# Group norms of a two-block forward pass: sums on all partitions, one chain per four groups, scales spread by single-pass matmuls

## The chip, the cores and the metric

The kernel runs on one core of a Trainium2 chip. The metric is the device time of one execution in microseconds (us). Before the change the median of three runs is 2449.47 us (2449.28 to 2449.51).

## What is computed

The reference runs a first transformer block (hybrid mixer and SwiGLU) and a second one on 256 tokens of width 2048, all in float32. Only one piece of the first block is touched by the change, the group norm behind the mixer:

```python
attn = forgetting_attention(q, k, v, log_f)            # 8 heads of 128
conv = gate_b * short_conv(gate_c * hc, conv_w)        # 8 groups of 128
y = jnp.concatenate([attn, conv], axis=-1).reshape(Bsz, L, N_GROUPS, GROUP_DIM)
y = rmsnorm(y, out_gain.reshape(N_GROUPS, GROUP_DIM)).reshape(Bsz, L, D_MIX)
return y @ w_out
# rmsnorm: y * rsqrt(mean(y * y, -1) + 1e-6) * gain
```

So each of 16 groups of 128 features needs, for each of 256 tokens, the mean of 128 squares, one over its root, and a product with it, before `w_out` can use the group.

## The kernel before, in words

Features lie on the 128 partitions and tokens on the free axis. `ytile[:, g, :]` is group g (heads are groups 0 to 7, the convolution's groups 8 to 15) as 128 features x 256 tokens. A sum over a group's features is therefore a sum over partitions, which TensorE makes by a matmul with ones.

**The dense products.** Every weight matrix streams through the ring `raw` (5 slots) in units of 128x1024. ScalarE rounds a unit to fp32r as `w_hi` (`split_hi`, L895), VectorE makes the rest `w_lo` (`split_lo`, L1307); both rings have 4 slots (`SPLIT`). A product is then made of single-pass fp32r matmuls of the two parts (L614 to L623). A product of a block of four output tiles is cut into *steps*: one unit for one of the four tiles (`product_step`), here 1536 or 1548 columns. In a step of "pair" tiles each second kind of matmul has 512 columns (L614, L618), in a step of "conv" tiles all have 258 (L621 to L623). Six PSUM banks (`out_bank`) take the tiles.

**The order of the rest** is written by hand as step numbers. Each engine's program walks through the steps; in step s it first does the work of the products (splits, evictions) and then what `rms`, `first_mixer` and so on hang on that step. Step numbers below count from CONV0, the first step of the convolution's products. Head hd has its scores at step 16 hd, its first and second transposes of the probabilities ("p0" and "p1", L703, L706) at 16 hd + 14, its product with v at 16 hd + 23 (L713 to L718). In `attention`, VectorE adds the masks and reduces (L1435 to L1442) one step behind the scores, ScalarE takes the exponentials (L958) three steps behind them, VectorE normalises (L1446, L1450) five behind.

**Side banks.** All these small matmuls write to two PSUM banks in turn. `take_side(kind, key, sem_free, value)` hands them out in program order; whoever takes a bank waits until the one that took it two places earlier has been read out:

```python
i = len(side_release)
if i >= 2:
    t_.wait_ge(*side_release[i - 2])
```

**The group norm before.** ScalarE squares a group (L981) into one of two buffers (`square_buf`) at `square_step[g]`. Three steps later TensorE sums it: two fp32 matmuls per group, with the squares as the stationary operand and one column of ones moving (L725), which leaves 128 tokens on the partitions x 2 columns. VectorE scales them into `gms` (L1454) a step later. When four groups have their sums, a *call* (`group_calls`, at a fixed step) makes the roots of all four at once on 128x8 elements: reciprocal (L1464), square root on ScalarE (L986), a Newton step in four small operations (`polish`, L1339 to L1345) two steps behind. Since the scales then lie with tokens on partitions, they are turned back in two *pairs* of groups: VectorE makes four diagonal 128x128 tiles (L1492), TensorE multiplies ones with them (four fp32 matmuls, L734) so that every partition has the scale of every token, VectorE multiplies `ytile` by that (L1473), ScalarE and VectorE split the result for `w_out` (L991, L1479). The four calls stand at steps 77, 108, 146 and 200; the spreads of their pairs (L734) 7 and 11 steps behind.

## Time and profile before

| | |
|---|---|
| median of 3 runs | 2449.47 us |
| profiled execution | 2449.89 us, its span 2447.8 us |
| TensorE matmul busy | 2433.8 us, 99% of the span |
| VectorE busy | 1614.5 us, 66% |
| ScalarE busy | 1202.2 us, 49% |
| GpSimd busy | 173.9 us, 7% |
| DMA engines, mean | 184 GB/s |
| TensorE clock granted, mean | 1.0 |
| spreads L734 | 64 records, 235.5 to 349.6 us |
| sums L725 | 64 records, 182.7 to 338.1 us |

Times count from the start of the span. An fp32 matmul stands as two records, an fp32r matmul or a transpose as one. Matmuls are pipelined and their ends are modelled, so what a piece of work costs TensorE is read from start to start. A difference of about 0.2% (4.9 us) is what a measurement of this kernel can tell from none.

### The profile page before, as it was taken

How to read it: one execution, taken by the hardware profiler on the slowest of the kernel's cores; microseconds unless marked ns; L12 is line 12 of the kernel's file. 1: busy time of each engine (PE TensorE's matmuls, PEld its weight loads, DVE VectorE, ACT ScalarE, POOL GpSimd, SP SyncE). 2: the span in 40 equal slices, each digit the busy share in tenths (PEclk: the TensorE clock that was granted, in tenths of full speed). 3: DMA queues.
4: the chain of work that ended last, by engine and by line, in shares of the span. 5: the costliest groups of instructions: out<-in, count | busy, mean ns of one | idle time of the engine just before them, and what ended most of it. 6: DMA issues, size and time to landing. Idle time of an engine off the chain costs nothing.

```text
span 2447.8 us, 36417 instructions
## 1 busy us (share of the span) xinstructions
PE 2433.8 (99%) x14762; PEld 2173.7 (89%) x14762; DVE 1614.5 (66%) x2518; ACT 1202.2 (49%) x1728; POOL 173.9 (7%) x195
## 2 busy tenths in 40 slices
PE   8999999999999999999999999999999999999999
PEld 8999998888888888888888888888998888888887
DVE  5646676676666666667677756678885665565667
ACT  6545545544544543455555654544554443443544
POOL 0001111000000000002211102031110000000010
PEclk9999999999999999999999999999999999999999
DMA  7554456666566666665655455565566666656663
GB/s 250 180 161 139 141 165 189 200 184 194 182 198 190 189 190 189 192 190 185 197 188 167 166 185 190 184 193 186 162 196 193 189 189 189 194 190 189 183 193 117
DMA packets 125751, 449.59 MB, mean 184 GB/s; under 512 B 13840, under 2 KB 16400, under 8 KB 125584
## 3 DMA queue, kind: packets, MB, share of 16 engines
q1 hardware_dynamic: 125296, 446.91, 58.8%
q8 instruction: 116, 1.90, 0.3%
q14 instruction: 51, 0.42, 0.0%
q10 hardware_dynamic: 288, 0.36, 0.0%
HBM read 445.12 MB, written 2.10 MB: 183 GB/s over the span
## 4 chain that ended last, share of the span: by engine, by line
PE 96%; DVE 2%; ACT 1%; issue 0%; DMA 0%; ACTq 0%
PE out_bank L614 28%; PE out_bank L618 27%; PE out_bank L615 14%; PE out_bank L617 14%; PE out_bank L622 3%; PE out_bank L621 3%; PE out_bank L623 3%; DVE w_lo L1307 1%; ACT w_hi L895 0%; PE side_bank L734 0%; PE side_bank L694 0%; PE side_bank L749 0%; PE side_bank L725 0%; DVE h L1824 0%; DMA h<-in_tokens 0%
## 5 line engine op out<-in xcount | busy, mean ns | idle before, releaser
L1307 DVE TENSOR_TENSOR w_lo<-raw,w_hi 128x1024 fp32r<-128x1024 f32 x839 | 1037.4, 1240 | 601.0 <-ACT w_hi L895 596.9
L895 ACT CAST w_hi<-raw 128x1024 fp32r<-128x1024 f32 x840 | 878.1, 1049 | 953.6 <-PE out_bank L618 874.8
L614 PE MATMUL out_bank<-a_op,w_hi 128*128 128x512 f32 x1984 | 784.2, 395 | 0.5 <-DVE h L1334 0.3
L618 PE MATMUL out_bank<-a_op,w_hi 128*128 128x512 f32 x1984 | 776.7, 391 | 0.0
L615 PE MATMUL out_bank<-a_op,w_lo 128*128 128x256 f32 x1984 | 558.8, 282 | 0.0
L617 PE MATMUL out_bank<-a_op,w_lo 128*128 128x256 f32 x1984 | 552.0, 278 | 0.0
L617 PEld LDWEIGHTS out_bank<-a_op,w_lo 128*128 128x128 f32 x1984 | 380.1, 192 | 84.3
L615 PEld LDWEIGHTS out_bank<-a_op,w_lo 128*128 128x128 f32 x1984 | 372.9, 188 | 77.0
L614 PE MATMUL out_bank<-b_op,w_hi 128*128 128x512 f32 x992 | 389.7, 393 | 0.0
L618 PE MATMUL out_bank<-b_op,w_hi 128*128 128x512 f32 x992 | 388.0, 391 | 0.0
L614 PEld LDWEIGHTS out_bank<-a_op,w_hi 128*128 128x128 f32 x1984 | 373.1, 188 | 2.0 <-DVE w_lo L1307 0.7
L618 PEld LDWEIGHTS out_bank<-a_op,w_hi 128*128 128x128 f32 x1984 | 373.0, 188 | 0.0
L615 PE MATMUL out_bank<-b_op,w_lo 128*128 128x256 f32 x992 | 279.7, 282 | 0.0
L617 PE MATMUL out_bank<-b_op,w_lo 128*128 128x256 f32 x992 | 275.8, 278 | 0.0
L617 PEld LDWEIGHTS out_bank<-b_op,w_lo 128*128 128x128 f32 x992 | 190.4, 192 | 42.0
L615 PEld LDWEIGHTS out_bank<-b_op,w_lo 128*128 128x128 f32 x992 | 186.3, 188 | 39.9
L614 PEld LDWEIGHTS out_bank<-b_op,w_hi 128*128 128x128 f32 x992 | 186.5, 188 | 0.0
L618 PEld LDWEIGHTS out_bank<-b_op,w_hi 128*128 128x128 f32 x992 | 186.5, 188 | 0.0
L1324 DVE TENSOR_TENSOR work<-work,out_bank 128x256 f32<-128x256 f32 x248 | 102.4, 415 | 119.0 <-ACT work L914 118.3
L621 PE MATMUL out_bank<-a_op,w_hi 128*128 128x258 f32 (+1 forms) x504 | 146.5, 291 | 0.0
L622 PE MATMUL out_bank<-a_op,w_hi 128*128 128x258 f32 (+1 forms) x504 | 144.2, 286 | 0.0
L623 PE MATMUL out_bank<-a_op,w_lo 128*128 128x258 f32 (+1 forms) x504 | 143.8, 285 | 0.0
(302 smaller groups left out, 1974.6 us busy)
## 6 DMA issues: line engine op xcount, KB each, us to landing
raw<-in_w_ff SPq DMA_DIRECT2D x256, 512.0 KB, 4.2
raw<-in_w_in SPq DMA_DIRECT2D x223, 512.0 KB, 3.7
raw<-in_w_gu SPq DMA_DIRECT2D x176, 512.0 KB, 4.2
raw<-in_w_down SPq DMA_DIRECT2D x88, 512.0 KB, 4.3
raw<-in_w_out SPq DMA_DIRECT2D x64, 512.0 KB, 4.3
raw<-in_w_ba SPq DMA_DIRECT2D x16, 512.0 KB, 3.9
raw<-in_w_bp SPq DMA_DIRECT2D x16, 512.0 KB, 3.8
out<-h SPq DMA_DIRECT2D x8, 256.0 KB, 2.3
```

The source lines that it names most:

```text
L614: t_.e.matmul(bank[:, :], wh, a_both, start=start, stop=False, skip_group_check=True)
L615: mm = t_.e.matmul(bank[:, 0:SEQ], wl, a_hi, start=False, stop=stop, skip_group_check=True)
L617: t_.e.matmul(bank[:, 0:SEQ], wl, a_hi, start=False, stop=False, skip_group_check=True)
L618: mm = t_.e.matmul(bank[:, :], wh, a_both, start=False, stop=stop, skip_group_check=True)
L621: t_.e.matmul(to, wh, a_hi, start=start, stop=False, skip_group_check=True)
L622: t_.e.matmul(to, wh, a_lo, start=False, stop=False, skip_group_check=True)
L623: mm = t_.e.matmul(to, wl, a_hi, start=False, stop=stop, skip_group_check=True)
L895: a.e.copy(w_hi[:, m % SPLIT, :], raw[:, u % RAW, :]).then_inc(hi_split)
L1307: v_.e.tensor_tensor(w_lo[:, m % SPLIT, :], raw[:, u % RAW, :], w_hi[:, m % SPLIT, :].bitcast(F32), ALU.subtract).then_inc(lo_split)
L1324: v_.e.tensor_tensor(y, y, bank_of(tile)[:, 0:SEQ], ALU.add).then_inc(bank_free)
```

## The change

The sum of a group is now one fp32 matmul with ones stationary and the 256 squares moving, so that all 128 partitions hold the sum of every token. VectorE scales 32 of the partitions into `group_ms`: the four groups of a call lie on partitions 0 to 31, 32 to 63, and so on. The chain of a call (reciprocal, square root, Newton step) runs on 128x256 elements, and two more operations split the scales into two fp32r parts, `scale_hi` and `scale_lo`. The diagonal tiles are gone: a pair is spread by four fp32r matmuls of 256 columns, whose stationary operand is one column of `group_pick` (a one on partition 0, 32, 64 or 96) repeated 128 times. Heads are summed 8 steps behind their square instead of 3; the first call moves from step 77 to step 82, the other three stay. A buffer for the DMA queues of GpSimd is made smaller (`dynamic_dma_scratch_size=8192`), and some waits follow the new semaphore counts.

```diff
--- before.py
+++ after.py
@@ -225,12 +225,15 @@
         cq = sb("cq", [P, 2, HEADS])
-        gms = sb("gms", [P, KT, 2])
         work = [sb(f"work{i}", [P, TOK]) for i in range(8)]
...
         minus = sb("minus", [P, 1])
+        group_ms = sb("group_ms", [P, 2, SEQ])
+        scale_hi, scale_lo = sb("scale_hi", [P, SEQ], F32R), sb("scale_lo", [P, SEQ], F32R)
+        group_pick = sb("group_pick", [P, 4], F32R)
+        group_y, group_z = work[6][:, 0:SEQ], work[7][:, 0:SEQ]
         ident = con[:, C_IDENT:C_IDENT + P]
...
@@ -402,7 +405,11 @@
 
-        group_calls = [(CONV0 + HEAD_STEPS * 4 + 13, (0, 1, 2, 3)),
+        sum_at, sums_at = {}, {}
+        for g in square_order:
+            sum_at[g] = square_step[g] + (8 if g < HEADS else 3)
+            sums_at.setdefault(sum_at[g], []).append(g)
+        group_calls = [(CONV0 + HEAD_STEPS * 4 + 18, (0, 1, 2, 3)),
                        (conv_tile["gate_b", 3].tau + 13, (8, 9, 10, 11)),
@@ -717,21 +724,21 @@
                                 skip_group_check=True).then_inc(attended)
-                for g in square_at.get(step - 3, ()):
+                for g in sums_at.get(step, ()):
                     i = square_no[g]
...
                     t_.wait_ge(y_squared, i + 1)
-                    for n in range(2):
-                        mm = t_.e.matmul(bank[:, n:n + 1], square_buf[i % 2][:, n * P:(n + 1) * P], ones[:, 0:1],
-                                         start=True, stop=True)
-                    mm.then_inc(y_summed)
+                    t_.e.matmul(bank[:, 0:SEQ], ones[:, :], square_buf[i % 2][:, :], start=True,
+                                stop=True).then_inc(y_summed)
                 if step - 3 in pair_at:
...
                     bank = take_side("groups", pair, group_normed, 2 * pair + 2)
-                    t_.wait_ge(group_diag, 4 * pair + 4)
-                    for i in range(4):
-                        diag = work[6 + i // 2][:, i % 2 * P:(i % 2 + 1) * P]
-                        mm = t_.e.matmul(bank[:, i * P:(i + 1) * P], ones[:, :], diag, start=True, stop=True)
+                    t_.wait_ge(group_step, 8 * c + 8)
+                    for i in range(2):
+                        one_row = group_pick[:, x + i:x + i + 1].to_broadcast([P, P])
+                        to = bank[:, i * SEQ:(i + 1) * SEQ]
+                        t_.e.matmul(to, one_row, scale_hi[:, :], start=True, stop=False)
+                        mm = t_.e.matmul(to, one_row, scale_lo[:, :], start=False, stop=True)
                     mm.then_inc(group_spread)
@@ -981,9 +988,8 @@
                     if step == at:
-                        n = 2 * len(groups)
-                        a.wait_ge(group_step, 6 * c + 1)
-                        a.e.activation(tiny[:, 1, 0:n], tiny[:, 2, 0:n], ACT.Sqrt).then_inc(group_step)
+                        a.wait_ge(group_step, 8 * c + 1)
+                        a.e.activation(group_y, group_z, ACT.Sqrt).then_inc(group_step)
                 if step - 5 in pair_at:
...
@@ -1405,6 +1411,7 @@
                     v_.e.tensor_tensor(pick, ident[:, H8], ident[:, 32:32 + HEADS], ALU.add).then_inc(pick_ready)
+                    v_.e.tensor_scalar(group_pick[:, 0:4], ident[:, 0:P:32], 1.0, None, ALU.mult).then_inc(group_pick_ready)
                 for tile in tiles_at(step, 1, "q"):
@@ -1448,22 +1455,33 @@
                         v_.e.tensor_scalar(pr, pr, r[:, i:i + 1], None, ALU.mult).then_inc(normed_p)
-                for g in square_at.get(step - 4, ()):
+                for g in sums_at.get(step - 1, ()):
                     i = square_no[g]
+                    c, x = divmod(y1_no[g], 4)
+                    at = slice(32 * x, 32 * x + 32)
                     v_.wait_ge(y_summed, i + 1)
-                    v_.e.tensor_scalar(gms[:, g, :], side_of["square", g][:, 0:2], 1.0 / P, RMS_EPS, ALU.mult,
-                                       ALU.add).then_inc(y_mean)
+                    if c >= 2:
+                        v_.wait_ge(group_step, 8 * (c - 2) + 8)
+                    v_.e.tensor_scalar(group_ms[at, c % 2, :], side_of["square", g][at, 0:SEQ], 1.0 / P, RMS_EPS,
+                                       ALU.mult, ALU.add).then_inc(y_mean)
 
...
                 for c, (at, gs) in enumerate(group_calls):
-                    n = 2 * len(gs)
-                    ms = gms[:, gs[0]:gs[-1] + 1, :].rearrange("p g i -> p (g i)")
-                    y, z = tiny[:, 1, 0:n], tiny[:, 2, 0:n]
+                    ms = group_ms[:, c % 2, :]
                     if step == at:
+                        if c == 0:
+                            v_.wait_ge(rms_spread, 1)
+                            v_.wait_ge(forget_step, 9)
                         v_.wait_ge(y_mean, max(square_no[g] for g in gs) + 1)
-                        v_.e.reciprocal(z, ms).then_inc(group_step)
+                        v_.e.reciprocal(group_z, ms).then_inc(group_step)
                     if step == at + 2:
-                        polish(ms, y, z, group_step, 6 * c + 2)
+                        polish(ms, group_y, group_z, group_step, 8 * c + 2)
+                        v_.wait_ge(group_step, 8 * c + 6)
+                        v_.wait_ge(group_spread, 2 * c)
+                        v_.e.tensor_scalar(scale_hi[:, :], group_y, 1.0, None, ALU.mult).then_inc(group_step)
+                        v_.wait_ge(group_step, 8 * c + 7)
+                        v_.e.tensor_tensor(scale_lo[:, :], group_y, scale_hi[:, :].bitcast(F32),
+                                           ALU.subtract).then_inc(group_step)
                 if step - 4 in pair_at:
@@ -1479,17 +1497,6 @@
                                                   ALU.subtract).then_inc(y1_split)
-                if step in pair_at:
-                    c, pair, x, gs = pair_at[step]
-                    v_.wait_ge(group_step, 6 * c + 6)
-                    if pair == 0:
-                        v_.wait_ge(rms_spread, 1)
-                    else:
-                        v_.wait_ge(group_spread, pair)
-                    for i in range(4):
-                        diag = work[6 + i // 2][:, i % 2 * P:(i % 2 + 1) * P]
-                        col = 2 * x + i
-                        v_.e.tensor_scalar(diag, ident, tiny[:, 1, col:col + 1], None, ALU.mult).then_inc(group_diag)
 
...
```

Three places of the instruction order are shown. In the rows, "waits" names the semaphores on which an instruction waits, and "xN" stands for N like rows.

The first is VectorE at the first call. Before, from the eviction of head 3's sum to the last of the first pair's diagonals:

```order
172 L1454 TENSOR_SCALAR gms<-side_bank 128x2 [waits y_summed]
173 L1464 RECIPROCAL tiny<-gms 128x8 [waits y_mean]
174 L1339 TENSOR_TENSOR tiny<-tiny 128x8 [waits group_step]
175 L1341 TENSOR_TENSOR tiny<-tiny,gms 128x8 [waits group_step]
176 L1343 TENSOR_SCALAR tiny<-tiny 128x8 [waits group_step]
177 L1345 TENSOR_TENSOR tiny<-tiny 128x8 [waits group_step]
178 L1307 TENSOR_TENSOR w_lo<-raw,w_hi 128x1024 [waits hi_split]
179 L1435 SCALAR_TENSOR_TENSOR probs<-side_bank,cq,masks 128x144 [waits p_turned,scored]
180 L1435 SCALAR_TENSOR_TENSOR probs<-side_bank,cq,masks 128x272
181 L1440 TENSOR_REDUCE soft<-probs 128x1 [waits masked] x2
182 L1442 TENSOR_SCALAR soft<-soft 128x2 [waits maxed]
183 L1492 TENSOR_SCALAR work<-con,tiny 128x128 [waits group_step]
```

and now, from the same eviction to the next unit's `w_lo` and the normalising of head 5:

```order
176 L1465 TENSOR_SCALAR group_ms<-side_bank 32x256 [waits y_summed]
177 L1476 RECIPROCAL work<-group_ms 128x256 [waits y_mean]
178 L1345 TENSOR_TENSOR work<-work 128x256 [waits group_step]
179 L1347 TENSOR_TENSOR work<-work,group_ms 128x256 [waits group_step]
180 L1349 TENSOR_SCALAR work<-work 128x256 [waits group_step]
181 L1351 TENSOR_TENSOR work<-work 128x256 [waits group_step]
182 L1481 TENSOR_SCALAR scale_hi<-work 128x256 [waits group_step]
183 L1483 TENSOR_TENSOR scale_lo<-work,scale_hi 128x256 [waits group_step]
184 L1313 TENSOR_TENSOR w_lo<-raw,w_hi 128x1024 [waits hi_split]
185 L1453 RECIPROCAL soft<-soft 128x2 [waits exped]
```

The call stood before the masks of head 5; it now stands behind them, in one piece of eight operations on 256 elements.

The second is ScalarE at the same place, now:

```order
178 L992 ACT_TABLE_LOAD
179 L992 ACTIVATE work<-work 128x256 [waits group_step]
180 L965 ACT_TABLE_LOAD
181 L965 ACTIVATE probs,soft<-probs,soft 128x144 [waits maxed]
182 L965 ACTIVATE probs,soft<-probs,soft 128x272
183 L902 CAST w_hi<-raw 128x1024 [waits unit_read,raw_landed3]
184 L902 CAST w_hi<-raw 128x1024 [waits unit_read,raw_landed4]
185 L979 COPY ytile<-side_bank 128x256 [waits attended]
186 L988 ACTIVATE acc<-ytile 128x256 [waits y_summed,y_attn]
187 L997 ACTIVATE b_op<-ytile,par 128x256 [waits group_normed] x2
188 L902 CAST w_hi<-raw 128x1024 [waits unit_read,raw_landed0]
189 L921 COPY work<-out_bank 128x256 [waits tile_done] x2
```

The square root (L992) and its table stood ahead of head 4's probability copies before; they now stand directly ahead of the exponentials of head 5, with no work between.

The third is TensorE at step 94, the transposes p0 and p1 of head 5, with the numbers of the banks. Before:

```order
1679 L623 MATMUL out_bank5<-a_op,w_lo 128x258
1680 L703 MATMUL side_bank1<-con,probs 128x128 [waits normed_p,group_normed]
1681 L703 MATMUL side_bank1<-con,probs 128x128
1682 L706 MATMUL side_bank1<-con,probs 128x128
1683 L703 MATMUL side_bank0<-con,probs 128x128 [waits y_mean]
1684 L703 MATMUL side_bank0<-con,probs 128x128
```

and now, with the four matmuls of pair 1's spread standing one step (six matmuls) ahead, into `side_bank1`:

```order
1673 L630 MATMUL out_bank5<-a_op,w_lo 128x258
1674 L710 MATMUL side_bank0<-con,probs 128x128 [waits normed_p,group_normed]
1675 L710 MATMUL side_bank0<-con,probs 128x128
1676 L713 MATMUL side_bank0<-con,probs 128x128
1677 L710 MATMUL side_bank1<-con,probs 128x128 [waits group_normed]
1678 L710 MATMUL side_bank1<-con,probs 128x128
```

p1 waited for the eviction of a sum (`y_mean`); it now waits for VectorE's products of `ytile` with pair 1's scales (`group_normed`), since the order in which the side banks are taken has changed. On VectorE, at this place, now:

```order
191 L1330 TENSOR_TENSOR work<-work,out_bank 128x256 [waits half_copied]
192 L1497 SCALAR_TENSOR_TENSOR b_op<-ytile,par,b_op 128x256 [waits y1_hi] x2
193 L1313 TENSOR_TENSOR w_lo<-raw,w_hi 128x1024 [waits hi_split]
194 L1526 TENSOR_TENSOR work<-out_bank,row 128x258 [waits y_conv,tile_done]
195 L1526 TENSOR_TENSOR work<-out_bank,row 128x258 [waits tile_done]
196 L1491 TENSOR_TENSOR ytile<-ytile,side_bank 128x256 [waits y_squared,group_spread]
197 L1491 TENSOR_TENSOR ytile<-ytile,side_bank 128x256 [waits y_squared]
```

The products of pair 1 (L1491) stand behind the evictions of three tiles that TensorE finishes in steps 92 to 94 (L1330, L1526), a split for pair 0 and a `w_lo`.

## Rows read from the trace of the kernel before

**Rows 1.** The page's chain that ended last, shares by engine.

```profile
PE 96%; DVE 2%; ACT 1%; issue 0%; DMA 0%; ACTq 0%
```

**Rows 2.** TensorE's waits: total us, times, longest us.

```profile
PE side_bank L703 <- DVE gms L1454: 0.5, 1, 0.5
PE side_bank L694 <- ACT probs_t L969: 0.5, 1, 0.5
PE side_bank L734 <- DVE work L1492: 0.4, 1, 0.4
```

**Rows 3.** Timeline of TensorE, an undisturbed spread: start us, duration us, instruction.

```profile
345.22 1.05 PE L734 MATMUL side_bank<-work,ones 128*128 128x128 f32 x8
...
346.82 0.40 PE L614 MATMUL out_bank<-b_op,w_hi 128*128 128x512 f32 x1
347.52 0.40 PE L614 MATMUL out_bank<-b_op,w_hi 128*128 128x512 f32 x1
```

**Rows 4.** The same view, an undisturbed sum.

```profile
337.81 0.50 PE L725 MATMUL side_bank<-ones,shift 128*128 128x1 f32 x4
...
338.96 0.41 PE L614 MATMUL out_bank<-b_op,w_hi 128*128 128x512 f32 x1
```

**Rows 5.** The same view, one fp32 matmul of 256 columns with ones.

```profile
1651.74 0.59 PE L774 MATMUL side_bank<-acc,ones 128*128 128x256 f32 x2
...
1652.87 0.39 PE L614 MATMUL out_bank<-a_op,w_hi 128*128 128x512 f32 x1
```

**Rows 6.** The same view, scores of heads 5 and 6, transposes of head 5.

```profile
231.16 0.41 PE L694 MATMUL side_bank<-k,q 128*128 128x144 f32 x2
...
246.00 0.38 PE L703 MATMUL side_bank<-con,probs 128*128 128x128 f32 x2
...
247.22 0.48 PE L614 MATMUL out_bank<-a_op,w_hi 128*128 128x512 f32 x1
...
249.41 0.51 PE L694 MATMUL side_bank<-k,q 128*128 128x144 f32 x2 [0.54 <-ACT probs_t L969]
```

**Rows 7.** Timeline of VectorE over the same stretch.

```profile
231.90 1.23 DVE L1307 TENSOR_TENSOR w_lo<-raw,w_hi 128x1024 fp32r<-128x1024 f32 x1 [1.36 <-ACT w_hi L895]
...
234.40 0.17 DVE L1442 TENSOR_SCALAR soft<-soft 128x2 f32<-128x2 f32 x1
...
245.01 0.42 DVE L1324 TENSOR_TENSOR work<-work,out_bank 128x256 f32<-128x256 f32 x1 [1.25 <-ACT work L914]
```

**Rows 8.** Timeline of ScalarE over the same stretch.

```profile
231.88 1.28 ACT L958 ACT_TABLE_LOAD   x1
234.60 0.41 ACT L958 ACTIVATE probs<-probs,soft 128x144 f32<-128x144 f32 x1 [1.43 <-DVE soft L1442]
...
235.52 1.03 ACT L895 CAST w_hi<-raw 128x1024 fp32r<-128x1024 f32 x1
...
238.85 0.91 ACT L991 ACTIVATE b_op<-ytile,par 128x256 fp32r<-128x256 f32 x2 [2.30 <-DVE ytile L1473]
```

**Rows 9.** Groups by line on VectorE: xcount, busy us, mean ns, idle before.

```profile
L1464 DVE RECIPROCAL tiny<-gms 128x8 f32<-128x8 f32 x4 | 0.8, 201 | 0.1
L1446 DVE RECIPROCAL soft<-soft 128x2 f32<-128x2 f32 x8 | 1.3, 158 | 0.0
```

**Rows 10.** Timeline of VectorE: a chain in which each waits for the one before.

```profile
460.11 1.34 DVE L1572 SCALAR_TENSOR_TENSOR work<-work 128x256 f32<-128x256 f32 x3
```

**Rows 11.** Timeline of VectorE behind the last call's first pair.

```profile
350.03 0.75 DVE L1473 TENSOR_TENSOR ytile<-ytile,side_bank 128x256 f32<-128x256 f32 x2 [0.26 <-PE side_bank L734]
350.70 1.22 DVE L1307 TENSOR_TENSOR w_lo<-raw,w_hi 128x1024 fp32r<-128x1024 f32 x1
351.84 0.87 DVE L1479 SCALAR_TENSOR_TENSOR b_op<-ytile,par,b_op 128x256 fp32r<-128x256 f32 x2
```

**Rows 12.** Timeline of TensorE at the start, steps of 272 columns.

```profile
6.49 0.57 PE L576 MATMUL out_bank<-a_op,w_hi 128*128 128x272 f32 x1 [6.49 <-DVE a_op L1312]
...
12.06 0.39 PE L621 MATMUL out_bank<-a_op,w_hi 128*128 128x272 f32 x1
```

More of the change, by code:

```diff
@@ L300, in two_blocks @@
         y_squared, y_summed, y_mean = sem("y_squared"), sem("y_summed"), sem("y_mean")
-        group_step, group_diag, group_spread, group_normed = (sem("group_step"), sem("group_diag"),
-                                                              sem("group_spread"), sem("group_normed"))
+        group_step, group_spread, group_normed = sem("group_step"), sem("group_spread"), sem("group_normed")
+        group_pick_ready = sem("group_pick_ready")
         gu_scaled, gate_silu, up_gated = sem("gu_scaled"), sem("gate_silu"), sem("up_gated")
@@ L1363, in rms @@
                         if r == 1:
-                            v_.wait_ge(group_spread, 8)
+                            v_.wait_ge(group_step, 32)
                         if r == 2:
@@ L2173 @@
     arrays = {n: np.ascontiguousarray(x) for n, x in arrays.items()}
-    nc = bacc.Bacc("TRN2", target_bir_lowering=False, num_devices=1)
+    nc = bacc.Bacc("TRN2", target_bir_lowering=False, num_devices=1, dynamic_dma_scratch_size=8192)
     aps = {n: nc.dram_tensor(n, x.shape, mybir.dt.from_np(x.dtype), kind="ExternalInput").ap()
```

## Prediction

> **What bounds the kernel.** I read the chain that ended last first: 96% of it is TensorE [rows 1]. TensorE waits for almost nothing; of its few waits in the whole run three lie in the stretch of the change, 1.4 us together, two of them on work that the change rewrites [rows 2]. So this edit can do two things only: change what TensorE itself spends on sums and spreads, and change who keeps it waiting between 158 and 355 us. VectorE's and ScalarE's extra work costs nothing as long as it ends before TensorE asks. The third view is therefore the timeline of the three engines around the first call, where the waits are.
>
> **Prices on TensorE, from start to start.** A step of 1536 columns takes 347.52 - 346.82 = 0.70 us. A spread of a pair with the step behind it takes 346.82 - 345.22 = 1.60, so 0.90 for the spread [rows 3]. A sum and its step take 338.96 - 337.81 = 1.15, so 0.45 [rows 4]. The new sum, one fp32 matmul of 256 columns with ones, exists already in the layer norm: 1652.87 - 1651.74 = 1.13, so 0.43 [rows 5]. The new spread is four single-pass matmuls of 256 columns, 1024 columns at the rate of a step: 0.47 [rows 3].
>
> - Spreads: 8 x (0.90 - 0.47) = **3.4 us gained**. No row shows a single-pass matmul with one repeated column as its weights by itself; the bounds are 0.47 and four times an fp32 one, 4 x 0.43 = 1.7. I take 0.47, since the operand's type is that of the dense products.
> - Sums: 16 x 0.02 = **0.3 gained**, as good as nothing.
> - Waits that go: p1 of head 5 waited for the eviction of a sum (0.5), pair 0's spread for its diagonals (0.4) [rows 2]. Sums of heads no longer stand between product and transposes: **0.9 gained**. The third wait, scores of head 6 behind ScalarE's copies of the probabilities (0.5), stays, since neither its bank nor ScalarE's order behind step 95 changes.
>
> Sum so far: -4.6 us. Now what becomes late.
>
> **Pair 0's spread (step 89).** On VectorE the chain of the call is now 128x256. Reciprocal: 158 ns for 2 elements and 201 for 8 [rows 9], 7.2 ns per element, so 0.20 + 248 x 0.0072 = 2.0 us. This is an extrapolation far beyond 8 elements; bounds are 0.46 (an ordinary operation of this size) and 2.3. Dependent operations of 256 elements stand 0.46 apart (3 in 1.34) [rows 10]; six of them 2.7 us. The chain starts when VectorE is through with head 5's masks, 234.40 [rows 7]: eviction to 234.8, reciprocal to 236.8, square root (about 0.45, as an exponential of this size [rows 8]) to 237.3, six operations to 240.1. The Trainium skill, "VectorE: DVE Perf Modes", section "First, the fixed hardware budget", says that the reciprocal is an iterative divide with a repeat count of 8; the small rows agree in kind. By it an element would cost eight times an ordinary one, 2.2 us in all, and this wait would be 0.2 longer.
>
> TensorE's arrival: from scores of head 5 (231.16) to p0 of head 5 (246.00) are 14.84 us [rows 6]; less the wait (0.4), two spreads (1.8) and a sum (0.45), 12.2 remain. It now starts 0.45 earlier, since head 3's sum is behind it: 230.7 + 12.2 + a sum 0.43 + two spreads 0.94 = 244.3 for p0; pair 0's spread lies two spreads and five steps ahead of that, 239.85. **Wait 0.3** (0 to 0.9).
>
> **p1 of head 5 (step 94), the main term.** In the new rotation of the two side banks p1 takes the bank of pair 1's spread, issued only one step earlier. It is free when VectorE has multiplied `ytile` by it. That work stands in VectorE's step 94, behind an eviction that needs step 94's product itself, and VectorE is late besides. Followed through:
>
> - ScalarE: square root done 237.3; the exponential's table 1.28, the exponentials 0.92 (234.60 to 235.52) [rows 8]: 239.5. Casts for two units, 1.0 each: 240.5, 241.5.
> - VectorE: `w_lo` waits for that cast, 240.6 to 241.7; normalising head 5, 0.7; next `w_lo` to 243.5; pair 0's products, the first by 243.9.
> - ScalarE: scales pair 0 (0.9) [rows 8], casts a unit (1.0), and only then copies half of the tile of step 92 (0.4): 246.2.
> - VectorE: joins that tile (0.35), splits pair 0 (0.85), `w_lo` (1.15), two evictions (0.75), pair 1's products (0.75) [rows 7, 11]: 250.0.
>
> TensorE is at p0 at 244.3 + 0.3 = 244.6 and wants p1 at 244.9. **Wait 5.1 us.** Lower bound: were VectorE as punctual as before, it would begin the join at 245.01 less the 1.4 us by which TensorE is earlier, 243.6, and end 3.85 later at 247.5: a wait of 2.6. Upper bound, with a reciprocal of 2.3 and small gaps: 5.7.
>
> No weight is late through this: a unit's `w_hi` and `w_lo` are made three units, twelve steps, ahead of use, over 8 us at 0.70 each, against a lateness of about 4.
>
> **The other calls.** Sum to spread is 11 steps at call 1, with a head's scores and transposes between: nothing (0 to 0.3), **0.1**. At call 2 it is 8 steps, 5.6 us, against eviction 0.4, reciprocal 2.0, root 0.5 and six operations 2.7, together 5.6 and some handovers: **0.5** (0 to 0.9). At call 3 it is 10 steps, 7.0 us, against 5.6 and one `w_lo` of 1.15: **0.1** (0 to 0.5). Behind call 3 the out product needs group 12 five steps behind the spread; the shorter spread moves both sides alike: 0. p1 of head 7 also takes the bank of a pair's spread, but seven steps behind it: covered. The four-column `group_pick` is one small operation 50 steps early, the smaller DMA buffer belongs to a queue that issues nothing here: 0.
>
> **Sum.** -4.6 + 0.3 + 5.1 + 0.1 + 0.5 + 0.1 = +1.5 us. The profiled execution took 2449.89 us, so 2451.4; it lies 0.42 above the median of the runs, so **2451.0 us**. Its own range, with all bounds: -4.9 + 2.6 to -4.2 + 0.9 + 5.7 + 0.3 + 0.9 + 0.5, that is 2447.2 to 2453.6. A measurement tells about 0.2% (4.9 us) from nothing: this is no change, made of two terms of five microseconds.
>
> **Rivals.**
>
> 1. *The long wait slows TensorE's clock; slower than before.* At the start, behind 6.5 us without work, the first 24 matmuls of 272 columns take 5.57 us, 0.23 each, which is 1.2 columns per ns, the lower level of 1.2 GHz [rows 12]; at the rate of a step they would take 3.0. If p1's wait does the same, it adds 2.6 us: 2453.6, and more if the low clock lasts longer; from 6 us at half rate on it is beyond 0.2%. For it: the wait is almost as long as the first one. Against: no wait within the run shows it, but none is longer than 0.5 us [rows 2]. Chance 0.17. The Trainium skill, "TensorE: Matmul & The Clock Gate", section "What's actually happening", states that the clock is gated to half when TensorE has been idle and released by activity; by it this rival is the rule and not the exception once the idle time is long enough.
> 2. *The wait at p1 is small, since VectorE and ScalarE are less late.* If the reciprocal costs like any operation of its size (0.46), the chain is 1.5 us earlier and the wait 3.6; with a punctual VectorE 2.6. Then 2447 to 2449.5. Chance 0.20.
> 3. *No collision at p1 at all.* Then only the gains and the small waits are left: 2449.47 - 4.6 + 1.0 = 2445.9, at the edge of what can be told. Against it stands the order of the rows: the bank is asked back within one step. Chance 0.05.
> 4. *The spreads are not single passes at full rate* (weights from one repeated column). At 1.7 each they cost 8 x 1.2 more: 2461. Chance 0.03.
>
> **How the numbers follow.** The forecast has 0.55. The range for 8 in 10 takes the forecast's own, most of rival 2 and rival 1 up to 3 us over it: 2446.5 to 2454.5. Faster by over 0.2% (below 2444.6) needs rival 3 with every bound at its best: 0.04. Slower by over 0.2% (above 2454.4): part of rival 1 and rival 4, 0.11. Within: 0.85.
>
> **What the profile would show.** Right: records of the new spread in four, about 0.12 us apart; sums as two records, 0.43 long; one long idle time of TensorE before the second group of transposes of head 5, near 245 us, released by VectorE's `ytile`; a reciprocal of 2 us; a short wait of the first and third call's spread for `scale_lo`; no wait of transposes for `group_ms`. Wrong: that idle time missing or under 2 us; matmuls 0.23 us apart behind it; idle time at a weight load behind it, which would mean that `w_lo` came late after all.

## Result and the profile after

The changed kernel takes 2453.31 us (median of 20 runs, 2452.86 to 2453.96), the kernel before beside it on the same chip 2449.64 (20 runs, 2449.18 to 2450.49): ratio 1.0015, 95% interval 1.0009 to 1.0021. That is 3.7 us slower, clear of noise and inside the 0.2% that the prediction calls no change. The profiled execution took 2453.19 us with a span of 2451.4, 3.6 us more than before.

The page of the changed kernel, totals and the shares of the chain that ended last:

```profile
span 2451.4 us, 36265 instructions
PE 2431.8 (99%) x14698; PEld 2171.7 (89%) x14698; DVE 1627.5 (66%) x2495; ACT 1202.3 (49%) x1728; POOL 173.0 (7%) x195
...
PE 95%; DVE 3%; ACT 1%; issue 1%; DMA 0%; SPq 0%; ACTq 0%; DVEq 0%
```

TensorE is 2.0 us less busy than before, the span is longer, and TensorE's share of the chain fell from 96% to 95% [rows 1]: what was won in its work was lost in waits, and in work at a lower clock. TensorE's waits (total us, times, longest us), the counterpart of [rows 2]:

```profile
PE side_bank L710 <- DVE ytile L1491: 6.0, 1, 6.0
...
PE side_bank L731 <- DVE group_ms L1465: 0.4, 1, 0.4
...
PE side_bank L740 <- DVE scale_lo L1483: 0.2, 1, 0.2
```

One wait of 6.0 us holds nearly everything; the three of before in this stretch are no longer listed. It stands in TensorE's timeline (start us, duration us, instruction, wait in brackets) where the prediction put it, at the second group of transposes of head 5 (L710):

```profile
242.77 0.28 PE L740 MATMUL side_bank<-scale_hi,group_pick 128*128 128x256 f32 x1
...
243.12 0.28 PE L741 MATMUL side_bank<-scale_lo,group_pick 128*128 128x256 f32 x1
...
243.96 0.43 PE L710 MATMUL side_bank<-con,probs 128*128 128x128 f32 x2
...
250.47 0.69 PE L710 MATMUL side_bank<-con,probs 128*128 128x128 f32 x2 [5.97 <-DVE ytile L1491]
...
252.24 0.42 PE L628 MATMUL out_bank<-a_op,w_hi 128*128 128x258 f32 x1
252.45 0.42 PE L629 MATMUL out_bank<-a_op,w_hi 128*128 128x258 f32 x1
...
255.42 0.28 PE L628 MATMUL out_bank<-a_op,w_hi 128*128 128x258 f32 x1
255.53 0.28 PE L629 MATMUL out_bank<-a_op,w_hi 128*128 128x258 f32 x1
```

Two things are to be seen. The four matmuls of pair 1's spread begin from 242.77 to 243.12, 0.12 us apart, and the bank that they write is asked back at 244.5 (250.47 less the wait of 5.97), 1.4 us after the last of them started. And behind the wait a matmul of 258 columns starts 0.21 us after the one before it at 252.45, but 0.11 at 255.53: the work in between ran at half speed. The granted clock says the same (the stretch and its length in us; busy us of PE, PEld, DVE, ACT and POOL; the clock as a share of full speed; DMA share, GB/s):

```profile
247.00:248.00 1.00, 0.00 (x0) 0.00 (x0) 1.00 (x2) 0.00 (x0) 0.86 (x2) 1.00 0.00 0
248.00:249.00 1.00, 0.00 (x0) 0.00 (x0) 1.00 (x1) 0.00 (x0) 0.01 (x1) 0.65 0.00 0
249.00:250.00 1.00, 0.00 (x0) 0.00 (x0) 1.00 (x4) 0.00 (x0) 0.16 (x1) 0.50 0.00 0
...
255.00:256.00 1.00, 1.00 (x8) 0.96 (x7) 0.96 (x3) 1.00 (x2) 0.00 (x0) 0.94 0.05 16
```

TensorE stands from 244.5 on. The clock is still at 1.00 (2.4 GHz) from 247 to 248, falls between 248 and 249 and is at 0.50 (1.2 GHz) from 249 on. Work starts again at 250.5 and runs at the low level until about 255.1: 4.6 us of work that would have taken 2.3.

From 245.74 to the end of the wait VectorE is busy. Its timeline:

```profile
234.57 1.75 DVE L1476 RECIPROCAL work<-group_ms 128x256 f32<-128x256 f32 x1
...
240.07 1.23 DVE L1313 TENSOR_TENSOR w_lo<-raw,w_hi 128x1024 fp32r<-128x1024 f32 x1 [0.81 <-ACT w_hi L902]
...
245.74 0.42 DVE L1330 TENSOR_TENSOR work<-work,out_bank 128x256 f32<-128x256 f32 x1 [1.84 <-ACT work L921]
246.08 1.34 DVE L1497 SCALAR_TENSOR_TENSOR b_op<-ytile,par,b_op 128x256 fp32r<-128x256 f32 x2
247.35 1.74 DVE L1313 TENSOR_TENSOR w_lo<-raw,w_hi 128x1024 fp32r<-128x1024 f32 x1
249.01 0.75 DVE L1526 TENSOR_TENSOR work<-out_bank,row 128x258 f32<-128x258 f32 x2
249.68 0.73 DVE L1491 TENSOR_TENSOR ytile<-ytile,side_bank 128x256 f32<-128x256 f32 x2
```

This is the order of work that was predicted, from the reciprocal (L1476) to the product that frees the bank (L1491, two operations in 0.73 us), which TensorE's wait names. In it VectorE itself waits 1.84 us, until 245.74, for ScalarE's copy of half a tile. ScalarE is late since the square root held up its exponentials and casts (in the run with the short chain below, the `w_lo` behind these casts starts at 238.08 and not at 240.07):

```profile
236.79 1.28 ACT L965 ACT_TABLE_LOAD   x1
...
239.01 1.99 ACT L902 CAST w_hi<-raw 128x1024 fp32r<-128x1024 f32 x2
...
244.42 1.03 ACT L902 CAST w_hi<-raw 128x1024 fp32r<-128x1024 f32 x1
245.35 0.36 ACT L921 COPY work<-out_bank 128x256 f32<-128x256 f32 x1
```

**The sum of the parts.** Prices: eight spreads and sixteen sums, -3.7. Waits between 158 and 355 us: 1.4 before, 6.6 now, +5.2. Half clock: +2.3. Together +3.8, against +3.6 by the spans. The difference arises wholly between the first scores of head 0 (158.92 before, 158.89 now) and the first scores of the second block's attention (1305.62 and 1309.22): +3.63. This distance is used below where two traces are compared, since it leaves out the start, where traces differ by up to about a microsecond whatever was changed.

### The profile page after: what moved, and what is told of

Its sections match the earlier page's. It is cut to its first block, busy times and chain, and to the rows that moved or that the text cites. A ratio compares the mean times of both kernels' runs of the same rounds, so it can differ in the third digit from the quotient of the medians.

```text
span 2451.4 us, 36265 instructions
## 1 busy us (share of the span) xinstructions
PE 2431.8 (99%) x14698; PEld 2171.7 (89%) x14698; DVE 1627.5 (66%) x2495; ACT 1202.3 (49%) x1728; POOL 173.0 (7%) x195
## 4 chain that ended last, share of the span: by engine, by line
PE 95%; DVE 3%; ACT 1%; issue 1%; DMA 0%; SPq 0%; ACTq 0%; DVEq 0%
PE out_bank L621 28%; PE out_bank L625 27%; PE out_bank L622 14%; PE out_bank L624 14%; PE out_bank L629 3%; PE out_bank L628 3%; PE out_bank L630 3%; DVE w_lo L1313 1%; ACT w_hi L902 0%; DMA raw<-in_w_in 0%; PE side_bank L731 0%; PE side_bank L756 0%; PE side_bank L701 0%; DVE h L1831 0%; SPq L477 0%
## 5 line engine op out<-in xcount | busy, mean ns | idle before, releaser
L1330 DVE TENSOR_TENSOR work<-work,out_bank 128x256 f32<-128x256 f32 x248 | 102.4, 415 | 120.1 <-ACT work L921 119.4
```

What stands on the lines that cost most here:

```text
L1330: v_.e.tensor_tensor(y, y, bank_of(tile)[:, 0:SEQ], ALU.add).then_inc(bank_free)
```

## Experiments

The question is not where TensorE waits but what a cure of it is worth, and how much of the 3.7 us each part carries: the moved order, the chain on 128x256, the half clock. The median of before was 2449.82 us beside the first four experiments, 2449.75 beside the next three and 2449.81 beside the last two.

**Pair 1's spread one step behind pair 0's**, so that its bank has five steps until it is asked back:

```
-                pair_at[at + 4 + x * 2] = (c, pair_base[c] + x // 2, x, groups[x:x + 2])
+                pair_at[at + 4 + (x // 2 if c == 0 else x * 2)] = (c, pair_base[c] + x // 2, x, groups[x:x + 2])
```

> The changed kernel (2453.3 us) with one edit: in the first call the second pair is spread one step behind the first (step 90) instead of four (step 93), so that its bank is asked back four steps later and not one. Theory A (the 6.0 us wait of p1 is the bank of pair 1's spread asked back one step behind, and the half clock behind it follows from the idle time): the wait falls under 0.5 us, the granted clock stays 1.0, time 2453.3 - 6.0 - 2.3 = 2445.0, up to 2446. Rival B (VectorE is behind by the longer chain and TensorE would meet that lateness wherever it next asks): the wait moves to another instruction, 2449 to 2453 us.

2450.10 us, ratio 1.0001 (0.9992 to 1.0010). The 6.0 us are gone and 3.2 us of the time with them, but not the 5.2 of added waits and the 2.3 of half clock: rival B of the expectation came true, and the waits moved. Five of them are left, 5.0 us together; the three longest:

```profile
248.05 0.51 PE L701 MATMUL side_bank<-k,q 128*128 128x144 f32 x2 [0.78 <-ACT probs_t L976]
255.60 0.70 PE L731 MATMUL side_bank<-shift,ones 128*128 128x256 f32 x2 [2.33 <-DVE probs L1442]
260.72 0.70 PE L731 MATMUL side_bank<-acc,ones 128*128 128x256 f32 x2 [1.20 <-DVE group_ms L1465]
```

A sum of this order waits for the masks of head 6, another for the eviction of the sum ahead. The long wait had hidden this: while TensorE stood still VectorE caught up. The clock stays up around the wait of 2.3:

```profile
254.00:256.00 2.00, 0.40 (x3) 0.38 (x3) 2.00 (x5) 0.00 (x0) 1.44 (x1) 1.00 0.28 16
```

**Matmuls of no use in the wait**, 24 fp32 ones of 128 columns between the two groups of transposes of head 5, into columns of the bank that nobody reads:

```
                         mm.then_inc(p_turned)
+                        if kt == 0 and hd == 5:
+                            for _ in range(24):
+                                t_.e.matmul(bank[:, 384:384 + P], ones[:, :], ones[:, :], start=True, stop=True,
+                                            skip_group_check=True)
```

> The changed kernel with 24 fp32 matmuls of ones with ones (128 columns, 0.21 us each, 5.1 us together) issued between p0 and p1 of head 5, into columns of the side bank that nobody reads. They fill most of the 6.0 us in which TensorE is idle and add nothing to the answer. Theory A (the idle time lowers the clock, worth 2.3 us): p1 starts at the same time as without them, no matmul behind it at half rate, granted clock 1.0, 2451.0 us. Rival (the slow matmuls behind the wait have another cause, or the filler delays p1): 2453.3 us or more.

2452.63 us, ratio 1.0012 (1.0003 to 1.0020), 0.7 us better than the changed kernel and 1.6 above the 2451.0 that theory A expected. The granted clock stays up over the same stretch, as expected, and yet:

```profile
248.00:250.00 2.00, 2.00 (x20) 2.00 (x19) 2.00 (x3) 0.00 (x0) 0.39 (x1) 1.00 0.03 10
250.00:252.00 2.00, 1.37 (x11) 1.10 (x10) 0.79 (x3) 0.00 (x0) 0.73 (x1) 1.00 0.74 195
```
```profile
250.85 0.44 PE L710 MATMUL side_bank<-con,probs 128*128 128x128 f32 x2 [0.63 <-DVE ytile L1495]
253.23 0.51 PE L701 MATMUL side_bank<-k,q 128*128 128x144 f32 x2 [0.54 <-ACT probs_t L980]
263.22 0.70 PE L735 MATMUL side_bank<-acc,ones 128*128 128x256 f32 x2 [1.11 <-DVE group_ms L1469]
```

The transposes start at 250.85, 0.4 us later than in the changed kernel. The fillers are not the reason: this trace is 0.4 late from the start (first scores of head 0 at 159.27 against 158.89). The work behind runs at full speed and meets two waits that the slow clock had covered: 0.5 at the scores of head 6, which the changed kernel does not list, and 1.1 where that had 0.4. So the half clock costs 2.3 us of matmul time but only 0.7 of kernel time by the medians, 0.9 from the scores of head 0 to those of the second block (1149.47 us against 1150.33): for the rest TensorE would have waited anyway.

**The chain on 8 columns.** Reciprocal, square root and Newton step work on 8 of the 256 columns, and the two parts of the scales are made from the means, so the kernel leaves the norm's scales out:

```
-                        v_.e.reciprocal(group_z, ms).then_inc(group_step)
+                        v_.e.reciprocal(group_z[:, 0:8], ms[:, 0:8]).then_inc(group_step)
...
-                        polish(ms, group_y, group_z, group_step, 8 * c + 2)
+                        polish(ms[:, 0:8], group_y[:, 0:8], group_z[:, 0:8], group_step, 8 * c + 2)
...
```

> The changed kernel with the reciprocal, the square root and the Newton step of every call on 8 of the 256 columns, and scale_hi and scale_lo made from the means instead of from the roots: the scales are left out, order and waits are the same. It shortens ScalarE's path to the exponentials by about 1.75 us and VectorE's chain by some 2.6. Theory A (a part of the wait, about 2.6 us by the prediction's lower bound, is in the order of the work and not in the length of the chain): the wait of p1 falls from 6.0 to about 4 us and is not gone; 2449 to 2451.5 us, the lower end if the clock stays up. Rival C (the wait is the length of the chain alone): wait under 1 us, 2445 to 2446 us.

2450.93 us, ratio 1.0004 (0.9995 to 1.0013). The wide chain costs 2.4 us; a wait of 4.3 is left though reciprocal, root and Newton step are short (0.17 to 0.20 us each on VectorE), as theory A expected, and the clock falls here too:

```profile
248.48 0.69 PE L710 MATMUL side_bank<-con,probs 128*128 128x128 f32 x2 [4.34 <-DVE ytile L1491]
```
```profile
248.00:250.00 2.00, 1.52 (x6) 1.43 (x7) 0.43 (x2) 0.00 (x0) 0.58 (x1) 0.59 0.81 262
250.00:252.00 2.00, 2.00 (x11) 1.65 (x9) 0.42 (x1) 1.44 (x5) 0.60 (x1) 0.56 0.00 0
```

**The order alone.** The kernel before, old sums, diagonals and chain, with the sums of heads 8 steps behind the square and the first call at step 82:

```
-        group_calls = [(CONV0 + HEAD_STEPS * 4 + 13, (0, 1, 2, 3)),
+        sum_at, sums_at = {}, {}
+        for g in square_order:
+            sum_at[g] = square_step[g] + (8 if g < HEADS else 3)
+            sums_at.setdefault(sum_at[g], []).append(g)
+        group_calls = [(CONV0 + HEAD_STEPS * 4 + 18, (0, 1, 2, 3)),
...
-                for g in square_at.get(step - 3, ()):
+                for g in sums_at.get(step, ()):
...
```

> The kernel before (2449.6 us) with two things from the change alone: heads summed 8 steps behind the square and the first call at step 82; old sums, old 128x8 chain, diagonals and old spreads. Theory A (the new rotation of the banks makes p1 wait for pair 1's products even with the short chain): a wait of about 2.7 us at p1 in place of the 0.5 before, 2451 to 2452 us. Rival C (the moved order alone is harmless): 2449.6 us or 0.9 less.

2453.35 us, ratio 1.0015 (1.0006 to 1.0024): the whole loss without one new instruction, and above the 2451 to 2452 that theory A expected, since that had no price for the clock. Its timeline and its clock:

```profile
240.42 1.13 PE L738 MATMUL side_bank<-work,ones 128*128 128x128 f32 x8 [1.04 <-DVE work L1496]
249.17 0.44 PE L707 MATMUL side_bank<-con,probs 128*128 128x128 f32 x2 [2.84 <-DVE ytile L1477]
```
```profile
249.00:250.00 1.00, 0.83 (x6) 0.79 (x7) 0.11 (x1) 0.00 (x0) 0.27 (x1) 1.00 0.72 201
...
250.00:252.00 2.00, 2.00 (x10) 1.71 (x9) 0.42 (x1) 1.58 (x5) 0.73 (x1) 0.54 0.39 154
252.00:254.00 2.00, 2.00 (x10) 1.77 (x10) 1.63 (x4) 1.96 (x4) 0.00 (x0) 0.60 0.00 0
```

The clock is lowered behind 2.8 us of waiting, but only when TensorE is at work again from 249.2 on (1.00 from 249 to 250, 0.54 from 250 to 252), while the wait of 2.3 us in the run with pair 1 early left it at 1.00. In this order the new arithmetic's 3.7 us on TensorE are paid back, since the wait at head 5 grows from 2.8 to 6.0 and the half clock lasts longer (from about 250.2 to 253.6 here, 3.4 us): the two kernels are equal to 0.1 us.

**The arithmetic alone**: the changed kernel with all sums 3 steps behind and the first call at 77 again:

```
-            sum_at[g] = square_step[g] + (8 if g < HEADS else 3)
+            sum_at[g] = square_step[g] + 3
...
-        group_calls = [(CONV0 + HEAD_STEPS * 4 + 18, (0, 1, 2, 3)),
+        group_calls = [(CONV0 + HEAD_STEPS * 4 + 13, (0, 1, 2, 3)),
```

> The changed kernel with its two shifts undone: heads are summed 3 steps behind the square and the first call is back at step 77; new sums, chain, split and spreads stay. The banks then rotate as in the kernel before. Theory A (the loss lies in the moved order: rotation and place of the call; the new arithmetic by itself gains): spreads -3.4 us, no p1 wait for pair 1; but the square root stands ahead of head 4's probability copies, so scores of head 5 wait about 1 us: 2446 to 2448 us against 2449.8. Rival C (VectorE's longer chain costs by itself, wherever it stands): 2450 us or more, with the lost time in waits for VectorE between 240 and 262 us.

2451.19 us, ratio 1.0005 (0.9996 to 1.0014). No gain: the median is 1.4 us above the kernel before, where theory A expected 2 to 4 less and rival C 2450 or more. The chain now lies ahead of head 5's masks on VectorE (its reciprocal starts at 230.66, the masks follow at 236.52), and scores, spread and transposes each wait:

```profile
233.69 0.51 PE L701 MATMUL side_bank<-k,q 128*128 128x144 f32 x2 [1.19 <-ACT probs_t L976]
242.69 0.38 PE L740 MATMUL side_bank<-scale_hi,group_pick 128*128 128x256 f32 x1 [0.57 <-DVE ytile L1491]
250.22 0.44 PE L710 MATMUL side_bank<-con,probs 128*128 128x128 f32 x2 [1.76 <-DVE group_ms L1465]
252.61 0.51 PE L701 MATMUL side_bank<-k,q 128*128 128x144 f32 x2 [0.54 <-ACT probs_t L976]
```

**The first call three steps later** (`+ 16`, step 80), sums 3 behind; and the same with **pair 1 at step 88**, as in the first experiment:

> As the one with both shifts undone, but the first call at step 80, its spreads at steps 87 and 91: the root then stands behind head 4's copies and the chain's second half behind the masks of head 5. Theory A: no wait for the root at scores of head 5 and none of p1 for pair 1, p0 of head 5 takes pair 1's bank three steps behind it (a wait of 0 to 2 us); 2446 to 2447 us. Rival C: 2450 us or more.

> As the call at step 80 with sums 3 steps behind, and pair 1's spread one step behind pair 0's (88 instead of 91). Theory A: the bank of pair 1 is free long before head 5's transposes; whatever wait of those is left in the version with step 91 goes; 2445.5 to 2446.5 us. Rival C (VectorE's load from 240 us on decides, as in the changed kernel with pair 1 early, where 2.3 us of wait came back at the sum of group 10): no better than with step 91.

2448.49 us, ratio 0.9995 (0.9986 to 1.0004), and 2447.92 us, ratio 0.9993 (0.9984 to 1.0002). Both are above what was expected of them (2446 to 2447 and 2445.5 to 2446.5). The early pair 1 is worth 0.6 by the medians, within the intervals. What is left in the second is four waits of transposes for the eviction of a sum just ahead:

```profile
PE side_bank L710 <- DVE group_ms L1465: 1.6, 4, 0.8
```

**The place of the call without the new arithmetic**: the kernel before with the first call at step 80, `+ 13` to `+ 16` and nothing else:

> The kernel before with nothing changed but the first call of the chain, at step 80 instead of 77 (old diagonals, old sums, sums 3 steps behind the square). It tells whether the gain of the version with lag 3, call 80 and an early pair 1 comes from the new arithmetic on TensorE or from the place of the first call. Theory A, the place of the call: pair 0's spread no longer waits for its diagonals (0.4), nothing else moves, 2449.0 to 2449.4 on a before of 2449.6; the new arithmetic then makes up the other 1.5 us of that version. Rival B, the arithmetic is worth nothing in place, as VectorE's later evictions give it back everywhere: the same place with the old arithmetic reaches 2448.0 to 2448.5 as well. Rival C: pair 0 and pair 1, three steps later, run into the sum of head 4 and the transposes of head 5, whose bank then waits for the pair's evictions as in the moved old kernel: 1 to 2.5 us of side bank waits near 246, 2450.5 to 2452.

2449.73 us, ratio 1.0000 (0.9991 to 1.0009). The place alone gains nothing, a little less than theory A expected (2449.0 to 2449.4): the diagonals' wait of 0.4 goes, that of the transposes grows from 0.5 to 1.0.

```profile
246.51 0.44 PE L703 MATMUL side_bank<-con,probs 128*128 128x128 f32 x2 [1.01 <-DVE gms L1454]
```

With the call at this same step the new arithmetic is 1.2 us faster (2448.49), a third of its 3.7. This compares medians taken at two times, whose kernels of before agree to 0.1 us, and the intervals overlap; the two traces give the same 1.2 from the scores of head 0 to those of the second block (1146.59 us and 1145.43).

**Sums of heads 4 to 7 alone 8 steps behind**, with call 80 and pair 1 early:

```
-            sum_at[g] = square_step[g] + (8 if g < HEADS else 3)
+            sum_at[g] = square_step[g] + (8 if 4 <= g < HEADS else 3)
```

> The changed kernel with the sums of heads 0 to 3 again 3 steps behind the square, those of heads 4 to 7 left 8 behind, the first call at step 80 and pair 1's spread at 88 instead of 91: against the version with all sums 3 behind it differs only in where the sums of heads 4 to 7 stand. Theory A: what is left of that version's waits, 1.6 us of transposes behind the eviction of a sum, falls for heads 4 to 7 and nothing takes its place: 2446.5 to 2447.5. Rival B: moved behind the transposes the sums take a place in the rotation of the banks that puts the sum of group 10 or 11 behind the masks of head 6, as it did with pair 1 early and the call at 82 (2.3 and 1.2 us of waits): 2449.5 to 2450.5, so that the distance of 8 steps itself is what doesn't pay, and not the place of the call.

2447.19 us (11 runs, 2446.62 to 2447.51), ratio 0.9989 (0.9980 to 0.9998): the one version that is faster than before with the interval clear of 1, 2.6 us under it and 6.1 under the changed kernel, as theory A expected (2446.5 to 2447.5). Its waits:

```profile
PE side_bank L731 <- DVE group_ms L1465: 0.6, 1, 0.6
PE side_bank L701 <- ACT probs_t L976: 0.5, 1, 0.5
PE side_bank L710 <- DVE group_ms L1465: 0.5, 2, 0.3
...
PE side_bank L740 <- DVE scale_lo L1483: 0.2, 1, 0.2
```

So sums of heads 4 to 7 behind the transposes seem to pay (0.7 us against all 3 behind, with intervals that overlap; 1.1 by the traces, 1143.83 us against 1144.94). From the first experiment, which has pair 1 early too, this version differs in two things: the first call stands at step 80 and not 82, and heads 0 to 3 are summed 3 steps behind their square. Which of the two keeps the 2.3 us wait away was not tried one by one.

## Why the prediction came out as it did

The time fell in the range and in the likeliest of the three outcomes (no change by the bound), but 2.3 us above the forecast, where rival 1 had put it. The range of 8 in 10 holds it since it was stretched to take in rival 1. That the range worked out from the forecast's own terms (2447.2 to 2453.6) holds it too is luck: it has no term for the clock. One of the prediction's own signs of being wrong, matmuls 0.23 us apart behind the wait, came true (0.21). By its steps:

- **Prices on TensorE.** Right. A spread is four starts 0.12 apart, 0.47. Between pair 6 and pair 7 the lag behind the kernel before shrinks by 0.42 (349.63 against 345.22 [rows 3], 352.93 against 348.94), against 0.43 expected per spread.
- **Waits that go.** The two named went. The third, scores of head 6 behind ScalarE's copies, was said to stay; the view of waits no longer lists it, as TensorE at half clock came later (253.68, while the copies began at 253.26). With fillers in place it is back with its 0.54.
- **Reciprocal.** 2.0 us estimated from 2 and 8 elements, 1.75 measured; per element 6.3 ns between 8 and 256 columns, where the small rows gave 7.2. The Trainium skill, "VectorE: DVE Perf Modes", section "First, the fixed hardware budget", has the reciprocal with a repeat count of 8, from which the prediction made an estimate of 2.2. The measurement is lower: an ordinary operation goes from 0.17 us at 8 columns to 0.43 at 256 (L1345 with the short and with the wide chain), 1.05 ns per element, so a reciprocal's element costs six ordinary ones.

```profile
L1476 DVE RECIPROCAL work<-group_ms x4: 1753/1753/1754, 234.6 to 344.1; 128x256 f32<-128x256 f32 x4
```

- **p1 of head 5.** Place, bank and releaser right; 6.0 us instead of 5.1, and beyond the upper bound of 5.7. VectorE ended at 250.4 instead of 250.0: it had gained 0.5 on the forecast by the time of ScalarE's copy (245.7 instead of 246.2) and then lost 0.9 in the last stretch, where the two splits took 1.34 instead of 0.87 [rows 11] and `w_lo` 1.74 instead of 1.22. TensorE was at its first transposes 0.6 us earlier than forecast (243.96), half of it since pair 0's spread did not wait. Both lengthen the wait. The lower bound of 2.6 has the same gap: in the run with the short chain VectorE began the join at 243.75, close to the 243.6 of that bound, but ended at 248.4 and not 247.5, with TensorE there at 244.1 and not 244.9, a wait of 4.3.
- **The other calls.** Pair 0's spread 0 instead of 0.3, call 2 0.2 instead of 0.5, calls 1 and 3 nothing instead of 0.1 each. Not foreseen: the sum of group 11 waits 0.4 for the eviction of the sum ahead of it.
- **The sum.** Prices and waits alone give +1.5 in the measurement as in the forecast; the small errors cancel. The step that failed is the choice that a long wait leaves the clock alone, a term that the forecast put at nothing; the runs showed half clock for 4.6 us, +2.3. That was rival 1, with 0.17, priced at 2.6 us and 2453.6: 2.3 and 2453.3 were measured. The argument against it, that no wait within the run showed it, was none, since no wait of the run before was longer than 0.5 us. The only long idle time in the rows, the first 6.5 us, was followed by matmuls at the rate of the low level [rows 12], and a forecast of a wait of 5.1 us should have followed that row. It was the weaker evidence, though: the granted clock of that stretch stands at 1.00 in the profile, and all 24 slow matmuls are of one place in the program (L576 to L578), so the place could have been the reason. The trace of the changed kernel rules the place out: there the same matmuls go from 0.23 to 0.12 apart in the midst, at 9.4 us. The Trainium skill, "TensorE: Matmul & The Clock Gate", section "What's actually happening", has the low level as the default and activity as what releases it. The traces agree in three kernels of this study (waits of 2.8, 4.3 and 6.0 us); in a fourth, with a wait of 2.3 us, the clock stayed at 1.00. (From 2451.0 the bound of 0.2% is 3.4 us away, so that rival 1 would have needed some 7 us at half rate to pass it, not 6.)
- **What rival 1 left out**: its price is not kernel time one to one. The filler run shows 0.7 us for it by the medians and 0.9 by the traces.
- **What the forecast did not ask**: which part carries the loss. The moved order alone gives all of it (+3.5); in that order the new arithmetic adds nothing on either side. The arithmetic alone, in the old order, gave no gain either (+1.4, within its interval).

## What to carry to other kernels

When one buffer of a short rotation is asked back one step after it was written, find the engine that frees it and add up everything in that engine's queue, not the chain alone: here the collision cost 6 us while 3.7 us had been won on the busiest engine. In three kernels here a wait of 2.8 us or more on TensorE also let its clock fall, but both the low clock and the wait are partly cover for engines that lag; take one away and price what is late next before counting on the gain. Undo a change's order and its arithmetic separately: here the new arithmetic gained in neither the moved nor the old order, though it took 3.7 us off the busiest engine, and a third order (first call at step 80, pair 1 close behind pair 0, only heads 4 to 7 summed late) made it a gain of 2.6 us.

## What the runs showed of the hardware

- TensorE's granted clock fell from 1.00 to 0.50 around waits of 2.8, 4.3 and 6.0 us in full work and stayed at 1.00 around one of 2.3 us. Around the 6.0 us it fell during the wait and came back 4.6 us after work had begun again; around the 2.8 us it fell only after work had begun again.
- VectorE and GpSimd sometimes lengthened each other where they worked at one time. The split of 128x1024 took 1.74 us from 247.35, with GpSimd at work from 247.29 to 248.01, and 1.23 at 240.07; two splits of 128x256 took 1.34 from 246.08, with GpSimd from 246.25 to 247.15, against 0.87 [rows 11]. In the kernel before it was the other way round: a split of 128x1024 that began at 245.35 took 1.22, and GpSimd's operation, begun at 245.51, took 1.64, where the same one in the changed kernel took 0.90 (from 246.25). And the two products L1491, which read PSUM, took 0.73 from 249.68 with GpSimd beside them from 249.84. That one engine is the cause of the other's length was not tested by itself.

```profile
245.51 1.64 POOL L1958 TENSOR_TENSOR work<-work,row 128x256 f32<-128x256 f32 x1 [26.35 <-DVE work L1324]
```

- A sum's eviction costs 0.42 us though it now has only 32 partitions of 256 columns, as much as an operation of 128x256 that reads PSUM (L1330, 0.42), and against 0.15 for the 128x2 of before: what counts here is the columns.

```profile
L1465 DVE TENSOR_SCALAR group_ms<-side_bank x16: 405/420/430, 190.2 to 343.6; 32x256 f32<-32x256 f32 x16
```

- Single-pass matmuls whose weights are one repeated column ran at the rate of the dense ones, 0.12 us for 256 columns.
